# A layer norm inside a fused transformer kernel: the variance as sums over a whole PSUM bank instead of four columns

## The reference

```python
def layer_norm(x, w, b, eps=LN_EPS):
    mu = jnp.mean(xf, axis=-1, keepdims=True)
    var = jnp.mean(jnp.square(xf - mu), axis=-1, keepdims=True)
    y = (xf - mu) * lax.rsqrt(var + eps)
    return (y * w + b).astype(x.dtype)

u = causal_depthwise_conv(a_half * jax.nn.sigmoid(b_half), conv_dw_w, conv_dw_b)   # 31 taps
u = jax.nn.silu(layer_norm(u, conv_ln_w, conv_ln_b))
y_conv = u @ w_conv_out
```

## Time and profile before

| | |
|---|---|
| Median of three runs | 1696.14 us (1695.92 to 1697.41) |
| Span of the profiled execution | 1694.9 us |
| PE busy | 1684.5 us, 99% |
| DVE, POOL, ACT busy | 874.7, 793.1, 706.1 us |
| Stage of the change (four gate tiles and the first w_conv_out pair) | about 1091.5 to 1127.2 us |

### The profile page before, as it was taken

The page is one execution under the profiler, slowest core; times in us unless marked ns, Lnnn a source line. Parts: engine busy times, 40 slices in busy tenths (PEclk is TensorE's granted clock), DMA queues, the critical chain, the costliest instruction groups (busy, mean ns, idle before and its releaser), DMA issues.

```text
span 1694.9 us, 21874 instructions
## 1 busy us (share of the span) xinstructions
PE 1684.5 (99%) x7963; PEld 1374.6 (81%) x7963; DVE 874.7 (52%) x1365; ACT 706.1 (42%) x977; POOL 793.1 (47%) x605
## 2 busy tenths in 40 slices
PE   9999999999999999999999999999999999999998
PEld 7777778788888888888878888788888888888887
DVE  6234374563616167797897878863355511101113
ACT  5333364431313134456464554784424422222232
POOL 2434354444545455543434344444545544654453
PEclk9999999999999999999999999999999999999999
DMA  5222222274636342233222332222222222332232
GB/s 187 99 75 74 74 104 82 81 261 157 229 117 225 122 151 100 93 106 125 100 100 101 117 104 99 99 75 99 76 99 100 76 98 99 129 127 91 99 124 100
DMA packets 32540, 193.84 MB, mean 114 GB/s; under 512 B 3648, under 2 KB 5696, under 8 KB 13792
## 3 DMA queue, kind: packets, MB, share of 16 engines
q1 hardware_dynamic: 25376, 158.89, 26.5%
q10 hardware_dynamic: 7104, 34.15, 5.8%
HBM read 190.86 MB, written 2.16 MB: 114 GB/s over the span
## 4 chain that ended last, share of the span: by engine, by line
PE 98%; DMA 0%; DVE 0%; ACT 0%; SPq 0%; issue 0%; DVEq 0%
PE gemm_bank L511 25%; PE gemm_bank L504 25%; PE gemm_bank L505 25%; PE gemm_bank L542 4%; PE gemm_bank L558 4%; PE gemm_bank L551 3%; PE gemm_bank L546 1%; PE gemm_bank L789 1%; PE aux_bank L975 1%; PE aux_bank L655 1%; PE aux_bank L980 1%; PE aux_bank L960 1%; PE aux_bank L681 1%; PE aux_bank L672 1%; DMA w_raw<-weights_dram 0%; PE aux_bank L953 0%
## 5 line engine op out<-in xcount | busy, mean ns | idle before, releaser
L454 POOL TENSOR_TENSOR w_lo<-w_raw,w_hi 128x512 fp32r<-128x512 f32 x580 | 771.5, 1362 | 881.6 <-ACT w_hi L1259 870.4
L504 PE MATMUL gemm_bank<-a_hi,w_hi 128*128 128x512 f32 x1008 | 402.6, 399 | 0.0
L505 PE MATMUL gemm_bank<-a_lo,w_hi 128*128 128x512 f32 x1008 | 393.2, 390 | 0.0
L1259 ACT ACTIVATE w_hi<-w_raw 128x2048 fp32r<-128x2048 f32 x145 | 276.5, 1907 | 187.1 <-PE gemm_bank L511 122.7
L504 PE MATMUL gemm_bank<-b_hi,w_hi 128*128 128x512 f32 x688 | 267.8, 389 | 0.0
L505 PE MATMUL gemm_bank<-b_lo,w_hi 128*128 128x512 f32 x688 | 267.7, 389 | 0.0
L511 PE MATMUL gemm_bank<-a_hi,w_lo 128*128 128x512 f32 x1024 | 258.7, 395 | 0.0
L511 PEld LDWEIGHTS gemm_bank<-a_hi,w_lo 128*128 128x128 f32 x1024 | 190.2, 188 | 45.0 <-issue 6.2
L504 PEld LDWEIGHTS gemm_bank<-a_hi,w_hi 128*128 128x128 f32 x1008 | 189.3, 188 | 43.9 <-issue 5.6
L505 PEld LDWEIGHTS gemm_bank<-a_lo,w_hi 128*128 128x128 f32 x1008 | 189.4, 188 | 39.4 <-issue 1.9
L2161 DVE SCALAR_TENSOR_TENSOR aux_bank<-scratch,gcol,aux_bank 128x511 f32<-128x511 f32 (+15 forms) x240 | 165.8, 734 | 14.2 <-ACT aux_bank L1485 11.9
(11 more groups left out here) (414 smaller groups left out, 2133.4 us busy)
## 6 DMA issues: line engine op xcount, KB each, us to landing
w_raw<-weights_dram SPq DMA_DIRECT2D x146, 1024.0 KB, 4.7
arena<-ada_dram ACTq DMA_DIRECT2D x32, 768.0 KB, 4.7
acc<-cum_rows ACTq DMA_DIRECT2D x8, 512.0 KB, 3.7
h<-x_t_dram SPq DMA_DIRECT2D x8, 256.0 KB, 5.9
row_b<-cum_rows ACTq DMA_DIRECT2D x4, 512.0 KB, 4.8
scratch<-cum_rows ACTq DMA_DIRECT2D x4, 512.0 KB, 4.2
out_t_dram<-a_raw SPq DMA_DIRECT2D x7, 256.0 KB, 2.2
w_raw<-weights_dram SPq DMA_DIRECT2D x4, 256.0 KB, 5.2
```

Source lines behind the costliest of these rows:

```text
L454: ins = pool.tensor_tensor(wlo[s][:, w], raw[s][:, w], whi[s][:, w].bitcast(F32), ALU.subtract)
L504: pe.matmul(gemm_bank[bank][:, :], whi[slot][:, w], hi[:, k, :], start=(n == 0), stop=False)
L505: pe.matmul(gemm_bank[bank][:, :], whi[slot][:, w], lo[:, k, :], start=False, stop=False)
L1259: act.activation(whi[panel % 2][:, :], raw[panel % 2][:, :], ACT.Copy).then_inc(w_hi_ready, 1)
```

## The change

The variance's product is made as the mean's already is: ones of 128x128 as the weights and ln_sum as the moving 128x512. Each of aux[0]'s partitions then holds the sums of all 512 tokens. ACT takes the root of the whole bank in place, DVE the reciprocal of the whole bank in place, and the eight multiplications read aux[0]. `spread(5)` and `inverse(5)` fall out, and with them one step of the semaphore r_ready, so later waits on it count one less. `gate_tile(2)`'s last two thirds come together. `group_sum(0)`, which writes aux[0] next, now waits for the eight multiplications.

```diff
             pe.wait_ge(ln_sum_step, 4)
-            token_sums((ln_sum,), sum_done)
-            gate_tile(2, (1,))
-            spread(5)
-            gate_tile(2, (2,))
+            pe.matmul(aux[0][:, :], ones[:, :], ln_sum, start=True, stop=True).then_inc(sum_done, 1)
+            gate_tile(2, (1, 2))
             gate_tile(3)
@@ group_sum
                 if m == 0:
-                    pe.wait_ge(root_ready, 6)
+                    pe.wait_ge(ln_raw, KC)
@@ ACT
             after(P_GATE, T_GATE)
-            roots(5, sum_done, 6, e=1)
+            act.wait_ge(sum_done, 6)
+            act.activation(aux[0][:, :], aux[0][:, :], ACT.Sqrt, bias=eps[:, 1:2], scale=1.0 / D).then_inc(root_ready, 1)
             load_table(ACT.Silu)
@@ DVE
-            inverse(5)
-            dve.wait_ge(r_ready, 6)
+            dve.wait_ge(root_ready, 6)
+            dve.reciprocal(aux[0][:, :], aux[0][:, :]).then_inc(rinv_ready, 1)
+            dve.wait_ge(rinv_ready, 6)
             dve.wait_ge(centered, KC)
             for k in range(KC):
-                dve.scalar_tensor_tensor(b_raw[:, k, :], conv_u[:, k, :], col("conv_ln_w", k), aux[1][:, :],
+                dve.scalar_tensor_tensor(b_raw[:, k, :], conv_u[:, k, :], col("conv_ln_w", k), aux[0][:, :],
                                          ALU.mult, ALU.mult).then_inc(ln_raw, 1)
```

More of the change, by code:

```diff
@@ L1042, in gate_tile @@
                     tile_low(0, P_GATE + j // 2, T_GATE + j, 0, blocks, a_hi, first=j % 2 == 0)
[L1044 to L1050, removed]
             gate_tile(0, (0, 1))
@@ L2424, in _ @@
             inverse(6)
-            dve.wait_ge(r_ready, 7)
+            dve.wait_ge(r_ready, 6)
             for k in range(KC):
@@ L2499, in result @@
             def result(n, chunks):
-                dve.wait_ge(r_ready, 8 + n)
+                dve.wait_ge(r_ready, 7 + n)
                 for k in chunks:
```

## The result

The changed kernel takes 1699.26 us (median of 20 runs, 1697.37 to 1700.23), the kernel before 1696.17 (20 runs, 1695.54 to 1697.41). The ratio is 1.0016, with a 95% interval of 1.001 to 1.0022: 1.7 to 3.7 us slower. The profiled execution took 1699.74 us, with a span of 1698.0.

A forecast was written before the change was run, and what follows sets the result against it. PE, busy for 99%, was taken as the bound; its 0.98 us gain is swallowed waiting for the last b_lo, leaving the chain's +1.35 us: span 1696.25, median 1697.5 us, 8-in-10 range 1695.2 to 1699.3.

The forecast's parts named there:

- PE's own time: Gate tile 2 on PE: two small steps removed, 1.87 us, one ones-product added, 0.89 us; net -0.98 us.
- The chain: ACT's root and DVE's reciprocal over 512 columns, up to b_lo: last b_lo released 1.35 us later, at 1128.01.
- DVE and POOL kept their distance: Last b_lo on DVE beside POOL's w_lo: both move 1.35 us, no change counted there; rival 4 otherwise, chance 0.03.
- The form of the stall: PE at its last b_lo pair: reaches it at 1125.63 and stands until 1128.0, some 2.4 us.
- The clock: PE's granted clock behind the b_lo stall: no cost in the sum; a fall was left to rival 3.
- Rival 3: PE's b_lo stall closes its clock to 1.2 GHz; fifteen slow products give +4.8 us, 1700.9 us; chance 0.04.
- The reason given against it: Kernel's end, against rival 3: PE idle for over 2.0 us before the clock fell, so such idleness is borne.
- The second reason: Against rival 3: PE stands at most 1.4 us between products anywhere now, after which the clock stayed 1.00.
- the forecast term: Delay of the chain to the last b_lo, which remains after the wait swallows PE's gain: +1.35 us.
- the whole stays within 0.2%: Whole kernel: no measurable difference, under about 0.2%, 3.4 us; chance 0.95, slower 0.04, faster 0.01.
- eight cycles a column: DVE's reciprocal by the skill page: 8.3 ns a column, 4.4 us for the bank; sum +2.4 us, 1698.5.

The follow-up runs named there:

- the profile whose clock stayed up: The changed kernel unaltered, one more profile: 1698.16 us in one execution, beside 1695.99 of the kernel before.
- 4, 256 and 512 columns: The changed kernel with its reciprocal over 4 or 256 of the 512 columns: 1695.53 and 1696.13 us; 512 is the changed kernel's own width.
- the filling: The changed kernel with eight unread identity transposes on PE ahead of each of the last two b_lo waits: 1697.79 us, ratio 1.0011.
- the second profile: The changed kernel run again unaltered, beside the others of its series on one chip: 1699.38 us, ratio 1.0016.

## Why the prediction was right, and where it was not

**PE's own time** was right: -0.96 us by the tile's window, forecast -0.98.

**The chain** was right in each link, and its +1.35 us are +1.27 in the stretch of the profile whose clock stayed up. Root 0.66 us (0.69); reciprocal 3.37 (3.39, off by 0.6%); the release of the last b_lo, counted from the start of the variance's product, 1128.19 - 1105.47 = 22.72 us against 1126.66 - 1105.22 = 21.44 before: +1.28, forecast +1.35. DVE and POOL kept their distance: the last three b_lo took 4.66 us together, and 4.69 before. That the wait swallows PE's gain showed at 4, 256 and 512 columns: 1695.5, 1696.1 and, with the clock held by the filling, 1697.8 us.

**The form of the stall** was half right. It was summed as one piece of 2.4 us at the last pair. It comes in two, since the seventh chunk is late as well; PE does two products between them. The prediction's own rows held this: the seventh b_lo began at 1123.1 and took 1.78 us, which with 1.35 more is 1126.2, while PE would reach its pair at about 1125.2. The end is the same.

**The clock** is the step that failed. The sum put the clock behind the stall at nothing. Rival 3 had the place and the direction, but it was given 4% and, for its 1700.9 us, fifteen slow products of 0.453 us; eight came, of 0.427. It happens in most executions, to judge by 1699.38 as the median of 11 runs whose profiled one shows the fall, beside 1698.16 in the one that doesn't, and by the 21 runs of 31 over 1699.0 us; and it costs eight products' worth, 1.6 us. The reason given against it, that the clock at the end of the kernel was still full after 2.0 us of idleness, was read wrongly: there, too, the clock fell some time after PE had stopped. Here it fell at about 1129.2, 1.0 us after PE had taken up work again, and in the second profile 0.1 us after. A clock that is still up at the end of a stall says nothing on whether it will stay up. The second reason, the stall of 1.37 us at 317 us after which the clock stayed up, was sound, but it is no more than one execution's row for a shorter stall. And the trace of before had a nearer row, which the prediction did not look at:

```profile
668.00:671.00 3.00, 3.00 (x26) 2.88 (x24) 2.25 (x6) 1.42 (x2) 0.00 (x0) 1.00 0.79 268
672.00:678.00 6.00, 6.00 (x26) 5.71 (x26) 3.26 (x10) 0.51 (x3) 6.00 (x6) 0.50 0.13 19
```

There the clock lies at 0.50 for 6.8 us, from 671.3 us on, behind small products with results of 128x1 and 128x2 and without any recorded wait of PE. All twelve profiles have a fall at this place, of 3.4 us in seven and of 6.8 in five, and that accounts for 0.8 to 0.9 us of the distance between executions ahead of the change. So a fall needs no stall as long as the 2.4 us that rival 3 argued about. Why the clock falls in one execution and not in another stays open.

The Trainium skill, page "TensorE: Matmul & The Clock Gate", section "A second HAM failure mode: psum-queue depth-cycling", tells of a like case, a kernel in which PE idles for short times between groups of products and the clock goes down and up; that section bore on this case more than the page's rule on one long gap.

Hence the number: 1697.5 was forecast and 1699.3 measured, just inside the upper end of the range. About 1.3 to 1.5 of the 3.1 us are the forecast term, 1.6 are the clock. That the number stayed in a range that was drawn without rival 3 is luck: with fifteen slow products, as rival 3 priced it, it would have left it. That the whole stays within 0.2% was given 95%, and 3.1 us is 0.18%. The prediction's reading of what the Trainium skill, page "VectorE: DVE Perf Modes", section "First, the fixed hardware budget", says of Reciprocal, eight cycles a column, would have given 1698.5 and been nearer to the median, but the reciprocal did not take 4.4 us; the nearness would have been an accident.

## What to carry to other kernels

Where one engine is busy for 99%, first look for the place where it meets its next operand with no slack: a saving on it is worth nothing there, and a step that grows on the side chain comes out nearly in full (3.37 us more on DVE gave 3.1 to 3.6). An operation whose time goes by columns (a reciprocal at 6.3 ns each) belongs on the smallest form of its data, even at the price of two small products and two hand-overs. A stall that cannot be avoided is best filled with products that are ready, which gave back 3.7 us here; and when a stall of PE is priced, the clock behind it is priced too, by eight products at half speed here, as something that occurs in a part of the executions. Single executions are compared over a stretch that holds the change, since the rest of their spans differs too.

## What the runs showed of the hardware

- A DVE reciprocal: 0.18 us for 4 columns, 0.96 for 128, 1.77 for 256, 3.37 for 512, the same line for SBUF and for PSUM in place.
- The granted clock fell to 0.50 behind two waits of 0.9 us each on PE, 0.7 us of work apart, 1.0 us after PE had taken up work again in one profile and 0.1 us after in another, and came back after 3.4 us; in a third profile of the same program it did not fall.
- It also fell in all twelve profiles at 671 to 674 us, behind small products (128x1 and 128x2) and with no wait of PE over 0.23 us there, for 3.4 or 6.8 us.
- Behind single waits of 0.6 us and 1.54 us (of PE's products), and behind three of 0.29, 0.96 and 0.95 us, it stayed at 1.00 in the profiles at hand.
- The subtractions b_lo = b_raw - b_hi on DVE followed one another at 0.61 to 0.65 us with POOL idle and took up to 1.78 beside POOL's subtraction.
